# A Conformer output projection as seven products of quarters instead of eight, with its weight sums on GpSimd

## What is computed

```python
def conformer_conv(h, w_in, b_in, dw_w, dw_b, ln_g, ln_b, w_out, b_out):
    val, gate = jnp.split(h @ w_in + b_in, 2, axis=-1)
    u = val * jax.nn.sigmoid(gate)
    u = depthwise_conv_centred(u, dw_w) + dw_b
    u = jax.nn.silu(layer_norm(u, ln_g, ln_b))
    return u @ w_out + b_out
...
        h = h + gt1 * rms_norm_2(y, g_mix_post[layer])
        f = swiglu_ffn(modulate_2(rms_norm_2(h, g_ffn_pre[layer]), sh2, sc2), w_ffn_in[layer], w_ffn_out[layer])
```

## Time and profile before

| what | value |
|---|---|
| time, median of 3 runs | 2522.62 us (2519.71 to 2524.5) |
| profiled execution: its time | 2516.73 us |
| profiled execution: its span | 2515.0 us |
| PE busy | 2114.5 us (84%) |
| DVE busy | 798.8 us (32%) |
| ACT busy | 342.1 us (14%) |
| POOL busy | 107.1 us (4%) |
| mean granted clock of TensorE | 0.95 of full speed |

### The profile page before, as it was taken

The page is one execution under the profiler, slowest core; times in us unless marked ns, Lnnn a source line. Parts: engine busy times, 40 slices in busy tenths (PEclk is TensorE's granted clock), DMA queues, the critical chain, the costliest instruction groups (busy, mean ns, idle before and its releaser), DMA issues. The chain is left out here.

```text
span 2515.0 us, 35384 instructions
## 1 busy us (share of the span) xinstructions
PE 2114.5 (84%) x15446; PEld 1237.1 (49%) x15446; DVE 798.8 (32%) x1386; ACT 342.1 (14%) x690; POOL 107.1 (4%) x123
## 2 busy tenths in 40 slices
PE   6999998576766775678889866689899999999999
PEld 2444755232322431244445532246586885667883
DVE  3474752010101110121222210046553435662124
ACT  3002420000100000010110000021452000232000
POOL 0001010000000000001111100000030000100000
PEclk9999999888878899989999998899999999999999
DMA  9777248999999999999999999983402895424442
GB/s 379 265 302 275 91 180 331 427 429 428 414 422 426 420 421 420 414 416 423 424 424 424 424 421 425 427 314 102 166 3 77 279 305 177 134 68 134 145 168 89
DMA packets 152283, 755.26 MB, mean 300 GB/s; under 512 B 13561, under 2 KB 77177, under 8 KB 103490
## 3 DMA queue, kind: packets, MB, share of 16 engines
q1 hardware_dynamic: 152130, 753.01, 75.1%
HBM read 751.92 MB, written 1.05 MB: 299 GB/s over the span
## 5 line engine op out<-in xcount | busy, mean ns | idle before, releaser
L1289 PE MATMUL psum<-ring,arena 128*32 128x320 f32 x4032 | 391.7, 507 | 188.9 <-DMA ring<-w_up_dram 105.0
L1380 PE MATMUL psum<-ring,arena 128*32 128x512 f32 x1344 | 222.4, 678 | 142.1 <-DMA ring<-w_down_dram 142.1
L772 PE MATMUL psum<-arena,ring 128*128 128x256 f32 x1408 | 304.5, 379 | 0.0
L1289 PEld LDWEIGHTS psum<-ring,arena 128*32 128x32 f32 x4032 | 130.9, 119 | 345.1 <-issue 150.8
L772 PEld LDWEIGHTS psum<-arena,ring 128*128 128x128 f32 x1408 | 267.3, 190 | 37.1 <-issue 0.8
L670 PE MATMUL psum<-ring,arena 128*128 128x512 f32 x480 | 213.3, 606 | 5.1 <-DVE arena L1941 2.6
L1380 PEld LDWEIGHTS psum<-ring,arena 128*32 128x32 f32 x1344 | 46.8, 120 | 298.8 <-DMA ring<-w_down_dram 212.5
L670 PEld LDWEIGHTS psum<-ring,arena 128*128 128x128 f32 x480 | 92.9, 195 | 123.0 <-issue 120.5
L2613 DVE COPY arena<-psum 128x512 f32<-128x512 f32 x16 | 11.1, 692 | 411.6 <-PE psum L530 411.6
L1296 PE MATMUL psum<-ring,arena 128*32 128x64 f32 x2016 | 123.9, 295 | 0.0
L1296 PEld LDWEIGHTS psum<-ring,arena 128*32 128x32 f32 x2016 | 79.5, 120 | 88.8 <-issue 79.3
(11 more groups left out here) (404 smaller groups left out, 2226.9 us busy)
## 6 DMA issues: line engine op xcount, KB each, us to landing
ring<-w_down_dram SPq DMA_DIRECT2D x82, 1536.0 KB, 20.0
ring<-w_gate_dram SPq DMA_DIRECT2D x78, 1376.0 KB, 17.8
ring<-w_up_dram SPq DMA_DIRECT2D x78, 1376.0 KB, 17.7
ring<-w_mod_dram SPq DMA_DIRECT2D x72, 1024.0 KB, 7.6
ring<-w_gate_dram SPq DMA_DIRECT2D x24, 2752.0 KB, 15.6
ring<-w_up_dram SPq DMA_DIRECT2D x24, 2752.0 KB, 15.1
ring<-w_down_dram SPq DMA_DIRECT2D x15, 3072.0 KB, 17.7
ring<-w_ffn_in_dram SPq DMA_DIRECT2D x88, 512.0 KB, 5.8
```

Of the source, the lines that this page charges most:

```text
L772: ins = nc.tensor.matmul(b[:, i * 256:(i + 1) * 256], ws[k // 4][:, k % 4, u, i * P:(i + 1) * P], R(XT + k * 256, 256), start=(k == 0), st ...
L1289: ins = nc.tensor.matmul(banks[u][c][32 * j:32 * j + 32, 0:GMAIN], x, w3[:, 64 * c:64 * c + 64, QGROUP * j:QGROUP * j + QGROUP], start=not ...
L1380: ins = nc.tensor.matmul(ybanks[half][32 * c:32 * c + 32, :], stationary, w, start=((half, c) not in begun), stop=(unit >= 36), skip_group ...
```

## The change

The Conformer's output projection goes over to the scheme of seven. A product now covers a pair of feature tiles (f = 0 to 3) and a quarter index j = 0 to 6. Weights come as four loads of 256 rows by 1024 columns where they came as four of 512 rows by 512 columns; both are 1 MB. The weight sums are made by POOL, which starts them when the input projection is done, since they use `XT` for t4. DVE makes the token sums, in the place where the squares lay. ACT runs Silu on the second token tile first, in the order (half 0, t 1), (half 0, t 0), (half 1, t 1), (half 1, t 0). The bias goes into three banks. The end of the branch takes the second half of token tile 0 first (`sooner` is 1).

```diff
+        def conf_token_tile(f, j):
+            at = SQ + f * 384
+            return R((CV + f * 512 + 128, CV + f * 512 + 384, at + 256, CV + f * 512 + 256, CV + f * 512, at,
+                      at + 128)[j], P)
+        def conf_weight_tile(w, f, j):
+            return R(XT + f * HALF, HALF) if j == 3 else weight_tile(w, f, j)
...
-            for t in range(TT):
-                for c in range(2):
-                    for k in range(KT):
...
-                        ins = nc.tensor.matmul(banks[t, c], R(CV + k * 256 + t * P, P), w[:, k % 4, :], start=False,
-                                               stop=(k == 7), skip_group_check=True)
...
+            for f in range(KT // 2):
+                enlist(("confo", f))
+                pe.wait_ge(slot_loaded[slot_of(("confo", f))], count_of[("confo", f)])
+                for j in (0, 1):
+                    pe.wait_ge(conv_out_ready, 8 * (f // 2) + 2 * (f % 2) + j + 1)
+                    conf_product(f, j)
+            for j in (5, 6, 4, 3, 2):
+                if j in JOINED:
+                    pe.wait_ge(products_joined, len(JOINED) + JOINED[j])
+                if j == 4:
+                    conf_product(0, 2)
+                for f in range(1 if j == 2 else 0, KT // 2):
+                    if j == 5:
+                        pe.wait_ge(conf_weight_sums_ready, f + 1)
+                        pe.wait_ge(conf_token_sums_ready, f + 1)
+                    conf_product(f, j)
...
+            for t in (1, 0):
                 rt = R(MU + t * P, P)
                 v.reciprocal(rt, rt).then_inc(vector_done, 1)
                 v.wait_ge(vector_done, tally.gave(vector_done))
...
+                normed_four(t, 0)
+            normed_four(1, 1)
+            normed_four(0, 1)
+            for f in range(KT // 2):
+                v.wait_ge(conv_out_ready, 8 * (f // 2) + 2 * (f % 2) + 6)
+                token_sums(f, conf_token_tile, conf_token_sums_ready)
+            join_products("confo")
+            end_and_begin(lambda t, c: product_in("confo", t, c), ZTF, 0, "f1", 8, 24, 1)
...
+            for h, t in ((0, 1), (0, 0), (1, 1), (1, 0)):
+                a.wait_ge(layer_norm_ready, tally.due(layer_norm_ready))
+                for f in range(4 * h, 4 * h + 4):
...
+            copy_first_product("confo")
...
+            g.wait_ge(bank_filled[bank_of(("conf", KT // 2 - 1, 1))], nth(("conf", KT // 2 - 1, 1)))
+            for f in range(KT // 2):
+                key = ("confo", f)
+                w = slot(slot_of(key))
+                g.wait_ge(slot_loaded[slot_of(key)], count_of[key])
+                b11, b21, b22, b12 = (conf_weight_tile(w, f, j) for j in (0, 1, 2, 6))
+                t1, t2, t4 = (conf_weight_tile(w, f, j) for j in (4, 5, 3))
+                g.tensor_tensor(t1, b12, b11, ALU.subtract).then_inc(conf_weight_summed, 1)
+                g.wait_ge(conf_weight_summed, tally.gave(conf_weight_summed))
+                g.tensor_tensor(t2, b22, t1, ALU.subtract).then_inc(conf_weight_summed, 1)
+                g.tensor_tensor(b12, b22, b12, ALU.subtract).then_inc(conf_weight_summed, 1)
+                tally.gave(conf_weight_summed)
+                g.wait_ge(conf_weight_summed, tally.gave(conf_weight_summed))
+                g.tensor_tensor(t4, b21, t2, ALU.subtract).then_inc(conf_weight_sums_ready, 1)
```

More of the change, by code:

```diff
@@ L1808, in _ @@
             rotating[0], turn[0] = ROTATING, turn[0] % ROTATING
-            banks = {(t, c): next_bank(("confo", c, t)) for t in range(TT) for c in range(2)}
+            for i, j in enumerate((0, 5, 6, 4, 1, 2, 3)):
+                next_bank(("confo", j), None if i < 6 else 7)
             for pair in range(KT // 2):
@@ L1827, in _ @@
-            for t in range(TT):
-                for c in range(2):
-                    for k in range(KT):
[L1830 to L1835, removed]
-                        ins = nc.tensor.matmul(banks[t, c], R(CV + k * 256 + t * P, P), w[:, k % 4, :], start=False,
-                                               stop=(k == 7), skip_group_check=True)
[L1838 to L1843, removed]
+            for j, c in ((1, 0), (3, 0), (4, 1)):
+                if nth(("confo", j)) > 1:
+                    pe.wait_ge(bank_drained[bank_of(("confo", j))], nth(("confo", j)) - 1)
+                nc.tensor.matmul(result(("confo", j)), const("ones")[0:1, :], R(E0 + 4096 + c * HALF, HALF)[0:1, :],
+                                 start=True, stop=False, skip_group_check=True)
@@ new lines, in conf_product @@
+            def conf_product(f, j):
+                key = ("confo", f)
+                ins = nc.tensor.matmul(result(("confo", j)), conf_token_tile(f, j),
+                                       conf_weight_tile(slot(slot_of(key)), f, j), start=(f == 0 and j in (0, 5, 6, 2)),
+                                       stop=(f == KT // 2 - 1), skip_group_check=True)
+                if f == KT // 2 - 1:
+                    ins.then_inc(bank_filled[bank_of(("confo", j))], 1)
+                if j == (SEVEN[-1] if f else 3):
+                    if f < KT // 2 - 1:
+                        ins.then_inc(weights_used, 1)
+                        frees(key, None)
+                    else:
+                        frees(key, ("confo", j))
@@ L2082, in heads_ss, with token_sums @@
                 v.wait_ge(vector_done, tally.gave(vector_done))
-            def token_sums(f):
-                a11, a12, a22, s1 = (token_tile(f, j) for j in (0, 1, 3, 4))
-                s2, s3, s4 = (token_tile(f, j) for j in (5, 6, 2))
+            def token_sums(f, tile, ready):
+                a11, a12, a22, s1 = (tile(f, j) for j in (0, 1, 3, 4))
+                s2, s3, s4 = (tile(f, j) for j in (5, 6, 2))
                 v.tensor_tensor(s3, a11, s1, ALU.subtract).then_inc(vector_done, 1)
@@ L2111, in weight_sums, with join_products @@
                 v.tensor_tensor(t4, b21, t2, ALU.subtract).then_inc(weight_sums_ready, 1)
[L2113 to L2115 removed]
+            def join_products(tag):
+                p = [result((tag, j)) for j in range(7)]
                 def filled(j):
[L2118 removed]
+                    v.wait_ge(bank_filled[bank_of((tag, j))], nth((tag, j)))
                 def joined(j, part):
@@ L2972, in _, with normed_four @@
             v.wait_ge(root_ready, tally.due(root_ready))
-            for t in range(TT):
+            def normed_four(t, h):
+                rt = R(MU + t * P, P)
+                four = R(CV + h * 4 * SEQ, 4 * SEQ).rearrange("p (f n) -> p f n", f=4)[:, :, t * P:(t + 1) * P]
+                v.tensor_tensor(four, four, bc(rt.unsqueeze(1), [P, 4, P]), ALU.mult).then_inc(layer_norm_ready, 1)
+            for t in (1, 0):
                 rt = R(MU + t * P, P)
```

72 lines of the change are left out of this document (33 added, 39 removed).

## The result

The changed kernel takes 2528.16 us (median of 11 runs, 2526.4 to 2534.34), the kernel before, run beside it, 2521.03 us (11 runs, 2514.53 to 2527.61). The ratio, taken over runs on the same chip, is 1.0036, 95% interval 1.0025 to 1.0046: 9.1 us slower (6.3 to 11.6). The two medians by themselves lie 7.1 us apart; the ratio is the better measure, and I go by it. The profiled execution took 2527.4 us, its span is 2525.6 us, 10.6 more than before.

The account below looks back on a forecast made before the run. PE was taken to set this stage's time, with DVE covered. The end -0.5, PE's wait for DVE +2.9 and clock +1.4 gave +3.8 us, set on the median 2522.62: 2526.4 us, range 2521.3 to 2531.0.

Parts of the forecast that it names:

- Where the time goes: POOL's weight sums delay DVE's convolution, PE idles 2.9 us in the mean's sums, lower clock adds 1.4: +3.8 with the end.
- the bounds: Limits on the whole change: at the least +1.9 us, at the most +8.2 us.
- The likeliest case: Whole kernel: +1.9 to +5.0 us, 2524.5 to 2527.6, chance 0.43; any outcome within 0.2% had 0.59.
- the first rival: Each POOL instruction locks DVE out for its whole 1.09 us; convolution loses 13.9 us, total +6.2, 2528.8 us; chance 0.33.
- The loss per weight sum: DVE's convolution beside POOL: 0.79 us lost for each of 14.5 weight sums, 11.5 us in all.
- the upper bound of 14.7: Most that DVE's convolution could lose to POOL's weight sums: 16 times 0.92 us.
- the cover: Slack between DVE's convolution end at 2235.54 and PE's need of its tiles at 2244.2: 8.7 us.
- The second rival: DVE's gapless convolution keeps POOL out, so only the end counts: -0.5 us, 2522.1 us; chance 0.17.
- The clock: PE's idle in the mean's sums lowers its clock behind it: 1.4 us lost, between zero and 2.6.
- The products and the end: 28 products end 3.8 us sooner, but the serial chain from join j = 4 to second diagonal leaves 0.5 us gained.
- The loads and the sums' own length: w_out and ffn1 loads cost zero; POOL's weight sums, 18 to 19 us until 2240, end before PE needs them at 2262.6.

Follow-up runs that it names:

- experiment 1: Changed kernel, with all sixteen weight sums on POOL held until DVE's convolution ends: 2519.88 us against 2518.34 before, ratio 1.0002.
- experiment 2: Kernel before the change, plus sixteen unused subtractions of 128x512 on POOL, started where the weight sums start: 2527.09 us, ratio 1.0042.
- experiment 4: Kernel before the change, plus 32 memsets of 128x512 on POOL at the weight sums' place, writing SBUF and reading nothing: 2521.48 us, one time.
- experiment 10: Kernel before the change, plus sixteen unused subtractions on POOL, started in the middle of DVE's last convolution run: 2523.02 us against 2518.69, ratio 1.0017.
- experiment 11: Changed kernel, with its sixteen weight sums released in the middle of DVE's last convolution run: 2520.46 us against 2518.63 before, ratio 1.0003.
- experiment 8: Changed kernel, with half the weight sums after the convolution and bias matmuls over 128 rows instead of one: 2518.17 us, ratio 0.9994 to before.
- experiment 5: Changed kernel, with seven filling matmuls on PE ahead of its wait for DVE in the mean's sums: 2527.47 us against 2517.71 before, ratio 1.0036.
- experiment 6: Changed kernel, with the weight sums of pairs 2 and 3 held until DVE's convolution ends: 2515.13 us against 2517.71 before, ratio 0.9992.
- experiment 7: Changed kernel, all weight sums after the convolution, norm and Silu in the old order, first token tile first: 2523.45 us against 2517.71 before, ratio 1.0026.
- experiment 3: Kernel before the change, plus eight unused subtractions of 128x512 on POOL, started where the weight sums start: 2520.4 us against 2518.34, ratio 1.0007.

## Why the prediction was right about the cause and too small

- **Where the time goes.** Right: DVE's convolution, then PE's wait inside the mean's sums, then low clock. Experiments 1 and 2 take that cause out and put it in alone, and both move the whole loss. 2526.4 us was forecast and 2528.16 measured, but against before it is +9.1 us and not +3.8, which is also above the +8.2 that the bounds gave at the most. That the absolute time still came within 1.8 us is luck: the change was forecast 5.3 us too small, but the old kernel's median was 1.6 us lower this time (2521.03 for 2522.62), and the two medians lie 2.0 us closer together than the ratio has it. The likeliest case, no change within 0.2%, was not what happened. It went as the first rival said, a longer lock.
- **The loss per weight sum** is the term that failed: 0.79 us times 14.5 forecast, 1.03 times 15 measured, 15.5 and not 11.5 us, above even the upper bound of 14.7. The step was "each 1.09 us where nothing is beside it": the row is a multiplication by a constant mask, and the sums are subtractions and take 1.27, as L3581 did in the same trace (experiment 1). With 0.18 more in the lock the same working gives 1.19 + 0.18 = 1.37 per turn; 1.43 was measured (0.40 + 1.03), and for the last 0.06 I have no term. PE's wait more than doubled (2.9 forecast, 6.6 measured), since all of what exceeds the cover goes to it; the cover, 8.7 us, was right.
- **What the rule would have given.** The whole instruction as the lock, with the right price, is 1.27 + 0.27 - 0.40 = 1.14 lost per sum, a little above the 1.03. The Trainium skill ("SBUF — State Buffer", "Who interferes with whom") has two more sentences that these runs bear out: a GpSimd instruction that only writes doesn't contend (experiment 4: 11.97 us beside 32 memsets), and issue order decides who blocks (the same sixteen subtractions cost DVE 15.4 us in experiment 2, started ahead of its last run, and nothing in experiment 10, started within it).
- **The second rival** was half right. A run of DVE under way does keep POOL out: 6.80 us for 1.27 in experiments 10 and 11, and in the changed kernel the first sum took 2.04 us, until DVE's run had ended at 2222.7. But behind that run DVE had a gap of 0.16 us and its pair from 2222.88, which reads PSUM; POOL got in there, and from then on the two took turns, instruction by instruction. The release fell 1 us before a gap that had thirty more of these instructions behind it; the prediction treated the question as one of DVE's pace, not of where the first sum falls. Two things aren't shown: whether the gap or the PSUM input let POOL in, and why a waiting POOL instruction gets its turn after every DVE instruction here, and after none of fourteen in experiment 10.
- **The clock.** 1.4 us forecast in the mean, 1.6 measured. The 1.7 at the products weren't forecast.
- **The products and the end.** Right: PE stands 2.35 us (2.3 forecast) before the first transposes, and the second diagonal ends 14.18 us (14.1) after the join of j = 4 starts. The 3.8 us that PE saves are given back to the serial end. The gain of 0.5 us was 0.1 at the most: 47.03 (experiment 11) for 47.13 before, 46.94 for 46.93 with the bias of full height, and 47.38 in experiment 1. A good part of the rest is that the first product starts 12.61 us after the mean's first instruction (experiment 11) and 12.67 before, where I had counted 0.3 less: PE then waits 0.72 us for ACT.
- **The loads and the sums' own length.** Right: no product waits for a slot or for a sum.

The sum as measured: 6.85 us for DVE (PE would have gone on 0.86 after its start, at 2244.57, and does at 2251.42), and 1.6 and 1.7 for the clock, are 10.15. Without them the stretch of 57.08 would be 46.93, which fits experiment 8 (46.94) and leaves 0.2 to the 47.13 of before; the difference is the 9.95. Of the span's 10.6, 0.65 lies outside of the stretch, of which 0.36 is a later start of the stage (2243.71 for 2243.35).

**Left open.** Whether the one-row bias lowers the clock. The clock fell at the bias, right behind it or at the first products in seven profiles with it (the changed kernel and experiments 2, 4, 5, 6, 7 and 10) and not in four (before, 1, 3 and 11), and in none of two with the bias of full height. That is no proof, and the medians don't show an effect. The low clock at the products can also not be called a cost of the change.

## What to carry to other kernels

POOL isn't free, however idle, if it reads SBUF beside a DVE instruction with two SBUF inputs: price the added instruction by a row of the same operation and operands, count what each costs the other engine, and set that sum against the other engine's cover. Where it starts matters as much: released within the last run of such DVE instructions it waited and hurt nobody (experiments 10 and 11); released just ahead of a gap with a run of thirty behind it, it took a turn with every instruction as long as it had work (experiments 2 and 3). And fewer matmuls were worth nothing here, where a serial chain behind them had been hidden under the very matmuls that were removed.

## What was not expected of the hardware

- POOL's first subtraction stood 5.5 us (6.80 - 1.27) behind an unbroken run of DVE's instructions of 0.48 us, and its later ones took turns with such instructions one by one.
- A subtraction of 128x512 on POOL takes 1.27 us, with two full operands (experiment 1) and with a constant as one of them (L3581); the multiplication by a constant mask takes 1.09. A memset of the size takes 0.58 (18.62 us for 32).
- The granted clock went to the 1.2 GHz level while PE was busy without a gap from 2253 on (experiment 4: 0.98, then 0.50).
